# Expert weights of a fused MoE layer in 2 MB transfers of 16 KB runs, with the down steps one up step later and the direct unit behind four staged ones

## The reference: what is computed

```python
logits = x2 @ w_router + b_router                  # 32 experts, top 4 of each token
gates  = softmax(top 4 logits)
# for each expert e, on the tokens routed to it:
gu  = xb @ w_up[e] + b_up[e]                       # (rows, 1024) @ (1024, 2048)
gate, up = minimum(gu[:, :1024], 7), clip(gu[:, 1024:], -7, 7)
act = (up + 1) * (gate * sigmoid(1.702 * gate))
out = act @ w_down[e] + b_down[e]                  # (rows, 1024) @ (1024, 1024)
y[token] += gate_weight * out                      # summed over the token's four experts
```

## Time and profile before

| | us |
|---|---|
| three runs of the kernel before: median (lowest to highest) | 1277.86 (1274.71 to 1279.33) |
| profiled execution, its own time | 1280.96 |
| profiled execution, span from the first to the last instruction | 1279.3 |
| TensorE busy in the span | 1164.8 (91%) |
| VectorE, GpSimd, ScalarE busy | 683.2, 652.6, 249.2 |
| mean granted TensorE clock | 0.975 of full |

### The profile page before, as it was taken

How to read it: one execution, slowest core, us unless ns; L and a number is a source line. 1 busy time by engine, 2 the same in 40 slices (tenths; PEclk the granted TensorE clock), 3 DMA queues, 4 the chain that set the end, 5 groups by cost and what they waited for, 6 DMA issues and landing times.

```text
span 1279.3 us, 30932 instructions
## 1 busy us (share of the span) xinstructions
PE 1164.8 (91%) x11113; PEld 584.7 (46%) x11114; DVE 683.2 (53%) x1256; ACT 249.2 (19%) x487; POOL 652.6 (51%) x709
## 2 busy tenths in 40 slices
PE   8999999999899989799897998998988979989895
PEld 7877777775433333333332333333433323333332
DVE  1999984121755545535542557355564445535634
ACT  2012124001222212122111221221212112212122
POOL 1012300000566768749671677496585756757772
PEclk9999999999999999999998999998999989989998
DMA  8973443346999999999999699999999999999996
GB/s 255 348 244 118 153 131 132 103 143 284 374 384 386 388 422 422 422 422 422 422 422 422 255 383 415 422 422 422 422 422 422 422 422 422 422 422 422 422 422 259
DMA packets 94540, 448.91 MB, mean 351 GB/s; under 512 B 8503, under 2 KB 42871, under 8 KB 45316
## 3 DMA queue, kind: packets, MB, share of 16 engines
q1 hardware_dynamic: 94078, 447.21, 87.2%
q10 hardware_dynamic: 437, 1.39, 0.3%
HBM read 447.00 MB, written 2.42 MB: 351 GB/s over the span
## 4 chain that ended last, share of the span: by engine, by line
PE 59%; DVE 20%; DMA 16%; issue 3%; DVEq 1%; ACT 1%; SPq 0%; ACTq 0%
PE banks L1372 21%; DMA ring<-in_w_down 15%; PE banks L1382 14%; DVE staging L803 8%; PE banks L1167 8%; PE banks L1089 4%; PE banks L1126 3%; PE banks L1147 3%; DVE hT L1036 2%; PE banks L1283 2%; PE banks L1133 2%; DVE hT L1029 1%; DVE hT L1026 1%; PE banks L1156 1%; DVE xq L334 1%
## 5 line engine op out<-in xcount | busy, mean ns | idle before, releaser
L524 POOL COPY ring<-staging 128x1024 f32<-128x1024 f32 x620 | 622.5, 1051 | 479.1 <-PE banks L1372 396.0
L1372 PE MATMUL banks<-ring,hT 128*32 128x512 f32 x3328 | 425.4, 606 | 8.2 <-DVE hT L779 7.6
L1382 PE MATMUL banks<-ring,hT 128*32 128x256 f32 x3328 | 231.1, 398 | 77.3 <-DMA ring<-in_w_down 50.0
L330 DVE TENSOR_TENSOR xt<-xt,banks 128x1024 f32<-128x1024 f32 x106 | 128.8, 1216 | 322.6 <-PE banks L1147 322.6
L1382 PEld LDWEIGHTS banks<-ring,hT 128*32 128x32 f32 x3328 | 109.7, 114 | 254.8 <-issue 153.3
L1167 PE MATMUL banks<-hT,ring 128*128 128x288 f32 x768 | 190.7, 410 | 0.0
L1167 PEld LDWEIGHTS banks<-hT,ring 128*128 128x128 f32 x768 | 146.5, 192 | 40.2
L1372 PEld LDWEIGHTS banks<-ring,hT 128*32 128x32 f32 x3328 | 100.6, 112 | 132.0 <-issue 97.7
L683 ACT COPY WT<-banks 128x256 f32<-128x256 f32 x52 | 19.4, 372 | 495.3 <-PE banks L1382 495.3
L803 DVE SCALAR_TENSOR_TENSOR staging<-staging 128x256 f32<-128x256 f32 x240 | 107.4, 522 | 0.0
L1026 DVE TENSOR_TENSOR hT<-banks,bupT 128x512 f32<-128x512 f32 x52 | 36.0, 692 | 130.6 <-PE banks L1089 130.6
(11 more groups left out here) (245 smaller groups left out, 739.0 us busy)
## 6 DMA issues: line engine op xcount, KB each, us to landing
staging<-in_w_up SPq DMA_DIRECT2D x248, 1024.0 KB, 17.5
ring<-in_w_down SPq DMA_DIRECT2D x66, 1024.0 KB, 10.6
staging<-in_w_down SPq DMA_DIRECT2D x62, 1024.0 KB, 17.8
ring<-in_w_in SPq DMA_DIRECT2D x24, 1024.0 KB, 10.0
ring<-in_w_up SPq DMA_DIRECT2D x8, 1024.0 KB, 4.8
ring<-in_w_branch_b SPq DMA_DIRECT2D x4, 1024.0 KB, 4.9
ring<-in_w_branch_a SPq DMA_DIRECT2D x4, 1024.0 KB, 5.0
ring<-in_w_out SPq DMA_DIRECT2D x4, 1024.0 KB, 4.9
```

The source lines that it names most:

```text
L330: nc.vector.tensor_tensor(dst, dst, rows, ALU.add).then_inc(y_added, 1)
L524: ins = nc.gpsimd.tensor_copy(ring[:, k, half], staged[k][:, half])
L1372: ins = mm(UP[g * BLK:(g + 1) * BLK, :], xT[:, k, :], ring[:, k, g * 512:(g + 1) * 512], start=k == 0, stop=k == UP_SLOTS - 1)
L1382: ins = mm(DN[q * BLK:(q + 1) * BLK, 0:256], actT[:, f % 4, f // 4, :], ring[:, UP_SLOTS + j, h * D + q * 256:h * D + (q + 1) * 256], star ...
```

## The change: what it does

1. Weights of an expert move in six units of 2 MB: four of w_up, two of w_down. A unit of w_up is 256 rows, two to a partition (16 KB in one run); a unit of w_down is 512 rows, four to a partition (16 KB in one run). Up to here row 128k+p lay in slot k; now row 256u+2p+h lies in slot 2u+h, so the transposes that make the other operand (of the tokens, of the activation, of the bias) and the norm's weights are taken in the same new order.
2. Semaphores: one per unit. A staged unit is free again when both its halves have been copied; GpSimd's copy of a half still adds to the count (8 of 16), so TensorE can start on the first half of a staged unit. The direct unit counts only as a whole.
3. SyncE's round: four staged up units of expert p+1, the direct unit of expert p (when all four down steps before it are done), then the staged down unit.
4. TensorE's loop: up 0, 1 and 2, the waits, then down 0, up 3, down 1, up 4, down 2, up 5, down 3, up 6, up 7, `combine(0)`.
5. Before the expert stage: one small transfer of the norm's weights more, two small transposes more, and expert 0's units are loaded in pairs of slots.

```diff
-AHEAD = 3
+AHEAD = 4
...
-    return a["w_up"][0, bass.ds(e, 1), k * P:(k + 1) * P, :].rearrange("e p n -> (e p) n")
+    return a["w_up"][0, bass.ds(e, 1), u * 256:(u + 1) * 256, :].rearrange("e (p h) n -> p (e h n)", p=P)
-    lo = (k - UP_SLOTS) * 256
-    return a["w_down"][0, bass.ds(e, 1), lo:lo + 256, :].rearrange("e (p h) n -> p (e h n)", p=P)
+    lo = (u - UP_UNITS) * 512
+    return a["w_down"][0, bass.ds(e, 1), lo:lo + 512, :].rearrange("e (p h) n -> p (e h n)", p=P)
...
-def load_staged_again(place, after, ks):
-    for k in ks:
-        sp.wait_ge(slot_full[k], place * 16 + 16 * (FILLS + 1))
-        load_staged(after, k)
-def load_last_slots(e, before):
-    for k in range(2 * STAGED, SLOTS):
-        sp.wait_ge(down_used, before * DOWN_SLOTS + (k - UP_SLOTS + 1))
-        load_slot(e, k)
+def load_staged_again(place, after, us):
+    for u in us:
+        sp.wait_ge(unit_full[u], place * 16 + 16)
+        load_staged(after, u)
+def load_last_unit(e, before):
+    sp.wait_ge(down_used, before * DOWN_SLOTS + DOWN_SLOTS)
+    load_unit(e, UNITS - 1)
...
-    load_staged_again(place, after, range(2 * AHEAD))
-    load_last_slots(here, before)
-    load_staged_again(place, after, range(2 * AHEAD, 2 * STAGED))
+    load_staged_again(place, after, range(AHEAD))
+    load_last_unit(here, before)
+    load_staged_again(place, after, range(AHEAD, STAGED))
...
     # GpSimd
-    ins = nc.gpsimd.tensor_copy(ring[:, k, half], staged[k][:, half])
-    ins.then_inc(slot_full[k], 16)
+    ins = nc.gpsimd.tensor_copy(ring[:, 2 * u + h, c * (SLOT // 2):(c + 1) * (SLOT // 2)],
+                                staged[u][:, lo:lo + SLOT // 2])
+    ins.then_inc(unit_full[u], 8)
...
     # TensorE
-def up(k, fills):
-    pe.wait_ge(slot_full[k], fills)
+def up(k, half, full):
+    pe.wait_ge(unit_full[k // 2], (half, full)[k % 2])
...
-def down(j, fills):
-    pe.wait_ge(slot_full[UP_SLOTS + j], fills)
+def down(j, half, full):
+    if j < 3:
+        pe.wait_ge(unit_full[UP_UNITS + j // 2], half if j == 0 else full)
...
-    up(k, after)
-    if k == 1:
+    up(k, after + 8, after + 16)
+    if k == 2:
         pe.wait_ge(act_ready, i + 1)
         pe.wait_ge(y_added, i * NT + 2)
-    if 1 <= k <= DOWN_SLOTS:
-        down(k - 1, here)
-    if k == 6:
-        pe.wait_ge(combT_ready, i + 2)
-        pe.wait_ge(out_ready, i + 1)
-        pe.wait_ge(y_added, i * NT + NT)
-        combine(0, row_out[0])
+    if 2 <= k < 2 + DOWN_SLOTS:
+        down(k - 2, here + 8, here + 16)
+pe.wait_ge(combT_ready, i + 2)
+pe.wait_ge(out_ready, i + 1)
+pe.wait_ge(y_added, i * NT + NT)
+combine(0, row_out[0])
```

More of the change, by code:

```diff
@@ L54 @@
 DOWN_SLOTS = SLOTS - UP_SLOTS
+UNITS = SLOTS // 2
 UNIT = 2 * SLOT
@@ L132, in hybrid_layer @@
         staging = sb("staging", [P, STAGED, UNIT])
-        staged = [staging[:, u, h * SLOT:(h + 1) * SLOT] for u in range(STAGED) for h in range(2)]
+        staged = [staging[:, u, :] for u in range(STAGED)]
         early = staging[:, 0:UP_UNITS, :].rearrange("p u n -> p (u n)")
@@ L152, in hybrid_layer @@
         mean_w = part(P)
+        ffn_rows = part(256, QN)
         xs_rows = spb[0:NS].rearrange("p g i -> p (g i)")
@@ L220, in hybrid_layer @@
         slot_full = [sem(f"slot_full{k}") for k in range(SLOTS)]
-        staged_full = [sem(f"staged_full{k}") for k in range(2 * STAGED)]
+        unit_full = [sem(f"unit_full{u}") for u in range(UNITS)]
+        staged_full = [sem(f"staged_full{u}") for u in range(STAGED)]
         slot_free = sem("slot_free")
@@ L278, in hybrid_layer @@
         dve_step, act_step = sem("dve_step"), sem("act_step")
-        NORM_MIX, GATE_A, GATE_B, B_B, CONV_B, LNC_G, LNC_B, NORM_FFN = range(8)
+        NORM_MIX, GATE_A, GATE_B, B_B, CONV_B, LNC_G, LNC_B, NORM_FFN, FFN_PAIRS = range(9)
         vec_names = ["norm_mix_g", "b_gate_a", "b_gate_b", "b_branch_b", "conv_b", "ln_conv_g",
@@ L366, in _ @@
                 load(vecrows[(4 + v) * KC:(5 + v) * KC, :], a[name][0].rearrange("(c p) -> c p", p=P), vec_in)
+            load(ffn_rows[:], a["norm_ffn_g"][0].rearrange("(q n) -> q n", q=QN), vec_in)
             for n in range(2):
@@ new lines, in load_unit, with load_staged @@
+            def load_unit(e, u):
+                sp.dma_start(ring[:, 2 * u:2 * u + 2, :].rearrange("p s n -> p (s n)"), unit_source(e, u)
+                             ).then_inc(unit_full[u], 16)
+            def load_staged(e, u):
+                sp.dma_start(staged[u], unit_source(e, u)).then_inc(staged_full[u], 16)
+            def load_staged_again(place, after, us):
+                for u in us:
+                    sp.wait_ge(unit_full[u], place * 16 + 16)
+                    load_staged(after, u)
@@ L422, in _ @@
+            def load_last_unit(e, before):
+                sp.wait_ge(down_used, before * DOWN_SLOTS + DOWN_SLOTS)
+                load_unit(e, UNITS - 1)
+            for u in range(UP_UNITS):
+                sp.wait_ge(*mix_block_used(MIX_BLOCKS - SLOTS + 2 * u + 1))
+                load_unit(0, u)
             sp.wait_ge(ya_evac, 2 * KC)
-            for k in range(UP_SLOTS):
-                load_staged(1, k)
+            for u in range(UP_UNITS):
+                load_staged(1, u)
             sp.wait_ge(*mix_block_used(MIX_BLOCKS - 1))
-            for k in range(UP_SLOTS, SLOTS):
-                load_slot(0, k)
@@ L428, in _ @@
-            for k in range(UP_SLOTS, 2 * STAGED):
-                load_staged(1, k)
+            for u in range(UP_UNITS, UNITS):
+                load_unit(0, u)
+            load_staged(1, STAGED - 1)
             sp.wait_ge(before_known, 1)
@@ L529, in _ @@
                 before = pool.value_load(items_before[0:1, bass.ds(place - 1, 1)], min_val=0, max_val=MAX_ITEMS)
-                for k in range(2 * STAGED):
-                    pool.wait_ge(staged_full[k], place * 16)
+                for u in range(UP_UNITS):
+                    pool.wait_ge(staged_full[u], place * 16)
                     pool.sem_inc(slot_free, 1)
[L533 to L536, removed]
+                    for h in range(2):
+                        pool.wait_ge(up_used, before * UP_SLOTS + (2 * u + h + 1))
+                        pool.sem_inc(slot_free, 1)
+                        copy_slot(u, h)
+                pool.wait_ge(staged_full[UP_UNITS], place * 16)
+                pool.sem_inc(slot_free, 1)
+                for h in range(2):
+                    pool.wait_ge(down_used, before * DOWN_SLOTS + (h + 1))
                     pool.sem_inc(slot_free, 1)
-                    copy_slot(k)
+                    copy_slot(UP_UNITS, h)
         @block.scalar
@@ L1095, in _ @@
                 if tt == 1:
-                    pe.wait_ge(vec_in, 16 * 8)
-                    tr(bank[7][:, 320:320 + 8 * KC], vecrows).then_inc(pe_early, 1)
+                    pe.wait_ge(vec_in, 16 * 9)
+                    tr(bank[7][:, 320:320 + 8 * KC], vecrows)
+                    pairs = ffn_rows[:].rearrange("q (p h) -> q h p", h=2)
+                    turned = bank[7][:, 320 + 8 * KC:320 + 9 * KC].rearrange("p (q h) -> p h q", h=2)
+                    for h in range(2):
+                        ins = tr(turned[:, h], pairs[:, h])
+                    ins.then_inc(pe_early, 1)
                 r = ROWS[tt]
@@ L1139, in turn_rows @@
                 turned = XB[:, 256:512].rearrange("p (q h t) -> p h q t", q=QN, h=2)
+                pairs = xg.rearrange("r (p h) -> r h p", h=2)
                 for h in range(2):
-                    ins = tr(turned[:, h], xg[:, h * P:(h + 1) * P])
+                    ins = tr(turned[:, h], pairs[:, h])
                 ins.then_inc(rows_turned, 1)
@@ L1198, in _ @@
                     pe.wait_ge(bup_in, 16)
-                    pairs = bup_rows.rearrange("e (b p h) -> e b h p", h=2, p=P)
+                    fours = bup_rows.rearrange("e (g p c) -> e g c p", c=4, p=P)
                     for f in range(2 * KC):
-                        ins = tr(bank[3][:, f * NE:(f + 1) * NE], pairs[:, f // 2, f % 2])
+                        ins = tr(bank[3][:, f * NE:(f + 1) * NE], fours[:, f // 4, f % 4])
                     ins.then_inc(small_turned, 1)
@@ L1389, in turn_raw @@
                 pe.wait_ge(raw_ready, i + 1)
-                pairs = raw.rearrange("t (b p h) -> t b h p", h=2, p=P)
+                fours = raw.rearrange("t (p c) -> t c p", c=4)
                 for c in range(4):
-                    ins = tr(TB[:, c * P:(c + 1) * P], pairs[:, c // 2, c % 2])
+                    ins = tr(TB[:, c * P:(c + 1) * P], fours[:, c])
                 ins.then_inc(raw_turned, 1)
@@ L1411, in _ @@
             for k in range(UP_SLOTS):
-                up(k, 16 * (FILLS + 1))
+                up(k, 16, 16)
                 if k == 3:
@@ L1428, in _ @@
             bodies = pe.value_load(n_bodies[0:1, 0:1], min_val=NE - 1, max_val=MAX_ITEMS - 1)
+            for u in range(UP_UNITS, UNITS):
+                pe.wait_ge(unit_full[u], 16)
```

(4 more changed lines are left out.)

26 lines of the change are left out of this document (9 added, 17 removed).

## The result

| | before | after |
|---|---|---|
| median of 12 runs (lowest to highest), us | 1279.05 (1274.71 to 1281.03, and one of 1458.57) | 1284.18 (1280.2 to 1289.85) |
| ratio, 95% interval | | 1.005 [1.004, 1.0061] |
| profiled execution: own time, span | 1280.96, 1279.3 | 1283.13, 1281.4 |
| mean granted TensorE clock | 0.975 | 0.964 |

A forecast was written before the change was run, and what follows sets the result against it. The prediction took the transfer queue as the mean limit; −11.0 + 3.2 + 3.4 − 3.4 = −7.8, plus 15 for a dry queue, gave +7.2 us and a median of 1285 us, range 1267 to 1297 (8 times in 10).

The forecast's parts named there:

- The run length: Weight transfers in both stretches: 16 KB runs make each slot 1.5% faster, −11.0 us over 290 slots (bounds 0 and −22).
- the line: DMA packet time fitted from 1 KB and 8 KB runs: 9.6 ns per packet plus 36.75 ns per KB.
- The direct unit counts as a whole: At the direct-slot stalls: TensorE waits for both slots, 2.45 us more each; +3.2 us net for two last stalls.
- the scale of the working: Times in the pair calculation, counted from 0 when the transfer queue reaches an expert's direct slots (794.9 us before the change).
- The direct unit is issued later: At both stretches' starts: direct issue waits for down 3 instead of down 2, 1.7 us each, +3.4 us.
- The second stretch: Later of two transfer-limited spans before the change, 762.91 to 1216.60 us; the first runs from 419.64 to 693.40.
- road into a dry queue: Either of two ways a pair empties the transfer queue: late staged issue or late direct issue, 2.2 to 2.3 us, overlapping.
- the pairs: Six places with two two-item experts in a row, two in the first stretch, four in the second, where the queue empties.
- Down steps one up step later: TensorE's loop: up 2 fills waits for VectorE, under 10 us left of 27.3; only −3.4 us counts, the rest lengthens stalls.
- The dry queue: At six pairs of two-item experts: the transfer queue empties, costing 2.5 us each, +15 us (6 to 22).
- the first pair: First two-item expert pair: its short stall grows longer and can drop TensorE's clock, 2 to 3 us.
- The sum: Whole kernel: −7.8 and +15 give +7.2 us, 1288.1 for the profiled execution, a forecast median of 1285 against 1277.9.

The follow-up runs named there:

- e10: Changed kernel with the direct unit split in two and each staged unit loaded as two 1 MB transfers with 8 KB runs; 0.9997 of the kernel before.
- e2: Changed kernel with the direct unit moved as two 1 MB transfers, each issued when its slot is free and waited for alone; 0.9892 of the kernel before.
- e9: Kernel of e8, but TensorE waits for both direct halves before down 2; 1.0049 of the kernel before.
- e8: Kernel of e2, but both direct halves are issued only after down 3; 0.9895 of the kernel before.
- e4: Kernel before the change with only TensorE's new step order, transfers as before; 0.9956 of the kernel before.
- e5: Changed kernel with an added SyncE wait that was already met, so the same work once more; 1.0025 of the kernel before.
- e6: Kernel of e2 with the direct unit behind three staged units instead of four; 0.9899 of the kernel before.
- e3: Changed kernel with TensorE's old step order (down 0 behind up 1, combine between up 6 and up 7); 1.0147 of the kernel before.

## Why the prediction was right, point by point

- **The run length.** Expected 428 GB/s and −11.0 us; seen 428, and e10's span is 10.5 us above e2's for ten of the twelve slots, where the line gives 9.5. The straight line through 1 KB and 8 KB held at 16 KB. The Trainium skill's 3 cycles per packet ("DMA: Bandwidth & Descriptors", section "Why small descriptors are slow (HBM only)") would have given 0.6%, and the trace has 1.5%: the rows decided rightly. Whether the transfers' size has a part in it was not tested.
- **The direct unit counts as a whole.** The stall was to end at +6.6 on the scale of the working. The queue starts again behind the staged issue at 745.08 and has twenty slots until it reaches the direct unit, so it does that at 745.08 + 2.2 + 20 x 2.447 = 796.2, and the stall ends at 802.72, +6.5. Right, and it is the cause of the loss: e9 against e8 puts 1.5% of the time on this one wait.
- **The direct unit is issued later: +3.4 us. Wrong**, by e8 it is nothing. The second stretch does not begin with that issue any more. The staged units asked for from 745.08 on now feed the queue until the direct issue at 764.65 (760 to 780 us is 1.00 busy where it was 0.89), and the pause lies ahead of them (0.93 busy from 740 to 760), since the first of them has to wait for GpSimd's copies of two slots, which begin at 740.90. So the stretch begins with the same road into a dry queue that the pairs have, which the forecast counted only in the pairs. The changed kernel's windows there (before, the second one moved 347 GB/s at 0.89, and the first 424):

```profile
740.00:760.00 20.00, 19.72 (x237) 8.06 (x233) 14.41 (x24) 3.67 (x8) 16.47 (x17) 1.00 0.93 376
760.00:780.00 20.00, 18.53 (x233) 8.12 (x229) 11.83 (x15) 3.41 (x7) 20.00 (x21) 1.00 1.00 428
```

- **Down steps one up step later.** Waits under 10 us: 8.5. e4 gave 0.9956 where −5.1 us of the same terms (waits and the step behind the stalls) make 0.996. That the other waits only lengthen stalls held too.
- **The dry queue.** Expected 2.5 us a pair (0.9 to 3.7), +15; measured 1.9, +11.7, and in e5 2.5, +14.9. The staged unit was to be issued at +40.6 and came at 835.64 − 796.2 = +39.4; the next direct one at +60.1, and came at +59.0. Both are some 1.1 us early. Most of it comes with TensorE's clock. After the stall its steps run for a while at a granted clock of 0.50, the lower level (1.2 GHz). Before the change that lasts until about 805, 5.9 us behind the stall's end (799.10); after it until about 807, 4.3 us behind the end (802.72) of a longer stall (7.93 us where it was 3.28). So 1.6 us less pass at half the clock, which is 0.8 us of steps, and the working had nothing for it. The windows, first before, then after (columns as in the earlier trace rows):

```profile
804.00:805.00 1.00, 1.00 (x12) 0.20 (x4) 0.00 (x0) 0.47 (x2) 0.96 (x1) 0.50 1.04 434
805.00:806.00 1.00, 1.00 (x16) 0.26 (x8) 0.00 (x0) 1.00 (x1) 0.10 (x1) 0.95 1.00 418
```

```profile
806.00:807.00 1.00, 1.00 (x15) 0.41 (x10) 0.00 (x0) 0.00 (x0) 0.44 (x1) 0.51 0.96 410
807.00:808.00 1.00, 1.00 (x20) 0.47 (x16) 0.00 (x0) 0.33 (x1) 1.00 (x2) 1.00 0.96 410
```

  For the first pair the forecast names 2 to 3 us of clock and adds them nowhere; the two pairs of the first stretch lost 2.3 us each, all causes together. A slip: the text says the staged unit would come some 20 us after the direct one; its own working says 12, and 12.1 it was.
- **The sum.** +7.2 forecast. With what was measured (0 for the issue instead of +3.4, 11.7 instead of 15) it would be +0.5; the profiled executions differ by 2.2 and the medians by 5.1. With e5's 14.9 it would be +3.7, where e5's profiled execution lies 3.5 above that of the kernel before. So the mechanism and the sign were right, but that 1285 came within 1 us of the median is in part luck: the term for the issue was too high by 3.4 us, and what makes up for it (2 to 5 us by the changed kernel's own profile, nothing by e5's) lies in differences between executions that no run explains. TensorE's mean granted clock is lower after the change (0.964 against 0.975), and all ten stalls there last 6.9 us or more; whether that is the rest was not tested.

e2, e6 and e8 beat both kernels: 1.0 to 1.1% below the one before. They keep the long runs for the ten staged slots, and let TensorE start on the first direct slot while the second is still landing.

## What to carry to other kernels

When transfers set the pace, the part to merge is the part that nobody waits for at once; the transfer on which an engine stalls should stay small, so that the engine can start on its first part. If it waits for the last byte (e9 against e8), everything that this engine frees comes later too. Before changing the grain or the order of a prefetch queue, work out its spare time at the tightest place (slots behind the next blocked issue times the time of one), for a full queue in the profile does not say how nearly it is empty. And a gain in rate is real only while the queue is fed: 1.5% of rate, 11 us, was here paid back by six pauses of about 2 us. All this was seen in one kernel.

## What the runs showed of the hardware that was not expected

A VectorE instruction that reads and writes on-chip memory (L1037, 128 x 256, 0.29 us alone and up to 1.14 us beside GpSimd's copies) took 8.04 us in e3, from 1109.62 to 1117.66, inside a run of twenty GpSimd copies without a gap between them (1097.76 to 1117.51). It ended when the run did. TensorE waited 7.57 us for the chain behind it. The same happened once more in that execution, 7.99 us from 1199.94, inside the next run of twenty copies (1188.03 to 1207.78), and TensorE waited 7.51 us.

The Trainium skill ("SBUF — State Buffer", sections "SBUF: two separate sides" and "Who interferes with whom") tells of an exclusive lock on the port pair that VectorE and GpSimd share: between a GpSimd instruction and a VectorE one that uses both ports, as this kind (`tensor_scalar`) can, whoever starts first has it for the whole instruction, and the other is blocked. By that the wait would be at most one copy, an estimated 1.05 us. Here about eight copies passed first, so the runs agree that GpSimd's copies hold VectorE up and not on the bound. In none of the other nine profiles of experiments, nor before or after the change, did this instruction take over 1.15 us, though they have unbroken runs of up to 24 copies (24.19 us from 759.48 in the changed kernel). What lets it happen was not tested, and e3 was profiled only once.
